# Context rows of the expert layer: ScalarE scales the value row in place, GpSimd adds it to the sum, VectorE keeps only the dot products

## The reference

```python
def peer_ffn(h, wq, keys, u, v):
    q = (x @ wq).reshape(n, PEER_HEADS, 2, PEER_DQ // 2)
    s = jnp.einsum('nhcd,hckd->nhck', q, keys)
    ... # per token: 8 heads x top 16 of 128 x 128 experts -> e (n x 128), softmax -> g
    def one(args):
        xb, eb, gb = args
        a = jax.nn.gelu(jnp.einsum('tkd,td->tk', u[eb], xb))
        return jnp.einsum('tk,tkd->td', (a * gb), v[eb])
```

## Time and profile before

| what | value |
|---|---|
| median of the runs | 4517.55 us (4517.3 to 4519.25) |
| span of the profiled execution | 4512.0 us |
| busy: PE / PEld | 3440.8 us (76%) / 1749.3 us (39%) |
| busy: DVE | 2848.3 us (63%) |
| busy: ACT | 1418.0 us (31%) |
| busy: POOL | 1434.5 us (32%) |
| moved by DMA | 1508.18 MB, 334 GB/s over the span |

### The profile page before, as it was taken

One profiled execution on the slowest core, in us unless ns is written; L12 is line 12 of the kernel. 1 busy time (PEld: TensorE's weight loads), 2 busy tenths in 40 slices (PEclk: granted clock), 3 DMA queues, 4 the chain that ended last, 5 costly groups with the idle time before them and its releaser, 6 DMA issues.

```text
span 4512.0 us, 39214 instructions
## 1 busy us (share of the span) xinstructions
PE 3440.8 (76%) x12464; PEld 1749.3 (39%) x12464; DVE 2848.3 (63%) x5950; ACT 1418.0 (31%) x4518; POOL 1434.5 (32%) x1306
## 2 busy tenths in 40 slices
PE   7888777666788778887777977788677777777776
PEld 3567554332443333432222466534232322323222
DVE  1227886777745765665675688758774675674544
ACT  2213554332223322222223345533222222222222
POOL 1000443233333333333333233222343343343332
PEclk9999788888999999999998988899899999999999
DMA  7443986668999999999997676556899999999997
GB/s 260 168 161 138 386 316 242 231 253 338 390 407 410 408 395 393 397 398 419 418 396 303 230 260 246 193 196 231 349 403 420 417 415 418 418 404 417 416 421 291
DMA packets 229119, 1508.18 MB, mean 334 GB/s; under 512 B 25392, under 2 KB 27440, under 8 KB 63920
## 3 DMA queue, kind: packets, MB, share of 16 engines
q0 software_dynamic: 185504, 1353.53, 75.2%
q1 hardware_dynamic: 43408, 152.14, 9.1%
HBM read 1501.38 MB, written 4.19 MB: 334 GB/s over the span
## 4 chain that ended last, share of the span: by engine, by line
DMA 34%; PE 33%; DVE 18%; ACT 8%; issue 6%; POOL 0%; SPq 0%; DVEq 0%; ACTq 0%; POOLq 0%
DMA work<-expert_dram,work 32%; PE psum L855 17%; DVE work L1688 5%; DVE work L1727 4%; PE psum L883 3%; PE psum L702 3%; PE psum L706 2%; DVE work L1737 2%; PE psum L770 2%; PE psum L795 1%; ACT work L1207 1%; ACT work L1220 1%; PE psum L754 1%; ACT work L1223 1%; DVE stat L1484 1%
## 5 line engine op out<-in xcount | busy, mean ns | idle before, releaser
L855 PE MATMUL psum<-work 128*128 128x512 f32 x4096 | 1958.6, 624 | 650.2 <-ACT work L1207 649.9
L1688 DVE SCALAR_TENSOR_TENSOR work<-work,psum 128x1024 f32<-128x1024 f32 x1024 | 1247.8, 1220 | 1026.3 <-DMA work<-expert_dram,work 1022.0
L1930 POOL DMA_INDIRECT work<-expert_dram,work x1024 | 995.6, 972 | 1726.9 <-PE psum L855 1683.1
L855 PEld LDWEIGHTS psum<-work 128*128 128x128 f32 x4096 | 767.7, 197 | 1804.9 <-ACT work L1207 1005.8
L1912 POOL DMA_INDIRECT work<-expert_dram,work x256 | 409.8, 1601 | 1209.4 <-DVE work L1727 804.8
L1198 ACT ACTIVATE work<-work 128x2 f32<-128x2 f32 x512 | 104.1, 203 | 1949.4 <-DVE work L1688 1949.3
L1727 DVE SCALAR_TENSOR_TENSOR work<-work 128x1024 f32<-128x1024 f32 x254 | 325.2, 1280 | 197.9 <-ACT work L1223 197.8
L1207 ACT ACTIVATE work<-const,work 128x128 f32<-128x128 f32 x1024 | 347.4, 386 | 0.7 <-PE psum L855 0.7
L1737 DVE SCALAR_TENSOR_TENSOR work<-work 128x1024 f32<-128x1024 f32 x256 | 311.8, 1218 | 11.7 <-DMA work<-expert_dram,work 11.7
L770 PE MATMUL psum<-work 128*128 128x128 f32 x1456 | 221.8, 312 | 73.2 <-ACT work L1130 60.6
L809 PE MATMUL psum<-work,ring 128*128 128x512 f32 x512 | 240.2, 625 | 28.1 <-ACT work L1077 28.1
(11 more groups left out here) (198 smaller groups left out, 2891.8 us busy)
## 6 DMA issues: line engine op xcount, KB each, us to landing
ring<-w_mod_dram SPq DMA_DIRECT2D x96, 512.0 KB, 5.2
ring<-w_in_dram SPq DMA_DIRECT2D x80, 512.0 KB, 5.3
ring<-w_query_dram SPq DMA_DIRECT2D x64, 512.0 KB, 5.5
work<-expert_dram,work POOLq DMA_INDIRECT x1280, 8.4
ring<-w_out_dram SPq DMA_DIRECT2D x32, 512.0 KB, 5.9
work<-rpb_dram POOLq DMA_DIRECT2D x2, 2688.0 KB, 12.3
xT<-xT_dram SPq DMA_DIRECT2D x1, 2560.0 KB, 11.2
work<-tables_dram POOLq DMA_DIRECT2D x2, 1024.0 KB, 5.4
```

The costliest lines, as they stand in the source:

```text
L855: last = pe.matmul(out[:, cols_], diag[:, n % NDIAG, :], rows[(SLOTS * t + s) % NBUF][:, D + 512 * half:D + 512 * half + 512], start=(s == ...
L1688: dve.scalar_tensor_tensor(u, u, 1.0, pair[0], ALU.mult, ALU.mult, accum_out=act_in[:, s:s + 1]).then_inc(dot_done, 1)
L1930: pool.indirect_dma_start(rows[m % NBUF], None, a[f"expert{l}"], bass.IndirectOffsetOnAxis(expert[:, t % 2, s:s + 1], 0)).then_inc(row_in[ ...
```

## The change

The weighted sum of step 4 leaves VectorE. ScalarE gets a fifth instruction for each slot: it multiplies the value row in its buffer by the coefficient, in place (128 x 1024), and waits for its own coefficient first. GpSimd then adds the scaled row to `csum` (a copy for slot 0). `ctx_work` on GpSimd issues what can be gathered, then an add, and after each add the gathers that this add makes possible. The rule by which a gather may be issued now looks at the adds that GpSimd has issued. VectorE's slot is the dot product alone.

```diff
@@ ScalarE, ctx_slots
                     act.activation(ccoef[:, one], ctanh[:, one], ACT.Identity, bias=chalf[:, one],
                                    scale=chalf[:, one]).then_inc(ctx_coef, 1)
+                    v = crows[CTX_BUF[l][0][s]][:, D:2 * D]
+                    act.wait_ge(ctx_coef, SLOTS * l + s + 1)
+                    act.activation(v, v, ACT.Copy, scale=ccoef[:, one]).then_inc(ctx_scaled, 1)
                     yield
@@ VectorE, ctx_slots
-                def add(s):
-                    v = crows[CTX_BUF[l][0][s]][:, D:2 * D]
-                    dve.wait_ge(ctx_coef, SLOTS * l + s + 1)
-                    if s == 0:
-                        last = dve.tensor_scalar(csum, v, ccoef[:, 0:1], None, ALU.mult)
-                    else:
-                        dve.wait_ge(ctx_added, SLOTS * l + s)
-                        last = dve.scalar_tensor_tensor(csum, v, ccoef[:, s:s + 1], csum, ALU.mult, ALU.add)
-                    last.then_inc(ctx_added, 1)
                 for s in range(SLOTS):
-                    if s:
-                        add(s - 1)
                     b = CTX_BUF[l][0][s]
...
-                add(SLOTS - 1)
@@ GpSimd
+            def ctx_add(l, s):
+                v = crows[CTX_BUF[l][0][s]][:, D:2 * D]
+                pool.wait_ge(ctx_scaled, SLOTS * l + s + 1)
+                if s == 0:
+                    last = pool.tensor_copy(csum, v)
+                else:
+                    pool.wait_ge(ctx_added, SLOTS * l + s)
+                    last = pool.tensor_tensor(csum, csum, v, ALU.add)
+                last.then_inc(ctx_added, 1)
+                ctx_sums[0] = s + 1
+            def ctx_work(l, calls, sums):
+                ctx_gather(l, calls)
+                while ctx_sums[0] < sums:
+                    ctx_add(l, ctx_sums[0])
+                    ctx_gather(l, calls)
...
-                    if s > calls + NBUF - 1 or (before[s] is not None and before[s] > calls - 2):
+                    if s > calls + NBUF - 1 or (before[s] is not None and before[s] >= ctx_sums[0]):
...
-                pool.wait_ge(ctx_added, SLOTS * l + 1 + max(s for s in range(SLOTS) if CTX_BUF[l][0][s] > 2))
+                outer = max(s for s in range(SLOTS) if CTX_BUF[l][0][s] > 2) + 1
+                ctx_work(l, calls, outer)
+                pool.wait_ge(ctx_added, SLOTS * l + outer)
                 pool.dma_start(keys, a["keysT"][l]).then_inc(keys_in, 16)
```

More of the change, by code:

```diff
@@ L535, in build @@
         ctx_coef = sem("ctx_coef")
+        ctx_scaled = sem("ctx_scaled")
         ctx_added = sem("ctx_added")
@@ L1893, in _ @@
         def _(pool):
-            ctx_next = [0]
+            ctx_next, ctx_sums = [0], [0]
+            def ctx_add(l, s):
[13 more added lines that the diff above has]
+                    ctx_gather(l, calls)
             def ctx_gather(l, calls):
@@ L1936, in _ @@
                 calls = 0
-                ctx_next[0] = 0
+                ctx_next[0] = ctx_sums[0] = 0
                 if l:
@@ L1958, in _ @@
                     if calls:
-                        ctx_gather(l, calls)
+                        ctx_work(l, calls, calls - 1)
                 for k in range(NPAIR):
@@ L1971, in _ @@
                     calls += ROW_CALLS[l]["Q"][s]
-                    ctx_gather(l, calls)
-                assert ctx_next[0] == SLOTS
+                    ctx_work(l, calls, calls - 1)
+                assert ctx_next[0] == SLOTS and ctx_sums[0] == SLOTS
                 gather(l)
```

2 lines of the change are left out of this document (removed).

## The result

The changed kernel is slower. It takes 4553.27 us (median of 6 runs, 4535.41 to 4574.58) against 4522.57 us of the kernel before in the same runs. The ratio is 1.007 with a 95% interval of 1.0043 to 1.0098. I had forecast 4490 us, which is 0.6% faster.

The account below looks back on a forecast made before the run. It took a loop of waits between VectorE and ScalarE, 3.73 us a slot, as the bound. Terms -10 - 5 + 0 - 13 - 5 + 0 + 2 + 4 = -27 us on 4512.0 gave 4485, plus 5.5 4490 us; range 4472 to 4508.

Parts of the forecast that it names:

- The place of the loop: Context slots: dot product, coefficient, sum and next dot product wait in turn on VectorE and ScalarE, 3.73 us a slot.
- the 250 that I had named: Sign of being right: ScalarE's waits for dot products fall from 522 us to under 250.
- relief in full: Rival: ScalarE's need alone decides; attention -32 and -29, out projection -9, queries -5; -75 us, 4443 us; chance 0.16.
- 2.0 to 2.7 us: Sign of being right: GpSimd's add takes about this long.
- The two paces, ScalarE's and GpSimd's: Attention, layer 0: ScalarE needs 8.6 us a step, GpSimd 8.5, against 9.67 us a step before.
- what is added on GpSimd: Step pricing GpSimd's 254 adds and 2 copies of 128x1024, beside its gathers: 3.75 us a slot.
- 1.738 x 1024/896 = 1.99 us undisturbed: GpSimd's add of 1024 columns, scaled from the same operation on 896 columns.
- I take 3.75, near the middle: GpSimd's time per slot in us, chosen between 3.3 at best and 4.1 with every dot product in the way.
- My upper end of 4.1: GpSimd's time per slot in us with every dot product in the way: 1.7 + 1.22 + (1.68 - 0.87) + 0.3.
- ScalarE's cost: Scaling on ScalarE, 1.05 us net; a slot costs 2.3 us, a step of attention in layer 1 6.6 us.
- slower: the shared path: Rival: GpSimd paces at 4.1 us a slot; attention, layer 0 unchanged, queries +25 and +7; about 4549 us; chance 0.24.
- the slower case: Outcome with GpSimd pacing, about 4549 us, chance 0.24; its sign was GpSimd with no idle time left in attention.

Follow-up runs that it names:

- the narrow add: The changed kernel with GpSimd's add cut to 64 of 1024 columns: 4420.95 us, ratio 0.9786 against the kernel before.
- the kernel without this: The changed kernel with attention's shares written as a tensor_scalar that also sums its output: 4532.15 us, ratio 1.0032 against the kernel before.

## Why the prediction was wrong

**Right.** The place of the loop: ScalarE's waits for dot products fell from 522 to 294 us, though not under the 250 that I had named, and the narrow add shows 4421 us, even below "relief in full". The add's length (2.356 us) lies in the "2.0 to 2.7 us" that I had named as a sign of being right, so that sign was too wide: the sum itself had 1.99. The scaling takes 1.148 us for 1.13. The two paces, ScalarE's and GpSimd's, were the right quantities to compare in attention of layer 0. Projection and out projection of layer 1 and the edge of the latent rows moved by less than 5 us.

**The step that failed** is "what is added on GpSimd", in two of its numbers:
- "1.738 x 1024/896 = 1.99 us undisturbed" is 2.356 us. The row it came from has an operand that is repeated eight times. The run with such an operand gives 1.970 us and 4497 us of time. I scaled by the number of elements and did not look at how the operands are read. The Trainium skill's "GPSIMD Engine Reference", section "3.1 Elementwise — side-by-side cycle accounting", has a figure for an add of two whole operands, 4497 ns for 2048 columns. Half of it, 2.25 us, is an estimate by that page, and it lies nearer to the trace than mine.
- "I take 3.75, near the middle" is 4.3 us. My upper end of 4.1 was built from 1.7 us of shared path; with the real add it is 2.36 + 1.21 + 0.82 = 4.4 us, and attention sits there, not in the middle: where GpSimd is the pace, dot products collect behind the add and run straight after it, in the way of the gather. The middle between "never meets" and "always meets" is no estimate for two engines in step. The sign that I had named for the slower case came: in 446 to 748 us GpSimd waits only 13.6 us in all for ScalarE (8.8 ahead of adds, 4.8 ahead of the first copy).

**What was missing:** the shares of attention. I listed dot products and the multiplications of the norm as what meets the adds. A tensor_scalar with one input I left out. The shares took 118 us more of VectorE in the two attention stages, and the kernel without this is about 21 us faster. In attention of layer 1 they and the dot products, not GpSimd's pace, lead the chain of waits: I had forecast -13 us there and 6.9 us more came.

**ScalarE's cost** was somewhat too small, which the other error hid: I had ScalarE at 6.6 us a step in attention of layer 1, and with the add over 64 columns the stage takes 279.4/40 = 7.0. The scaling costs 64 us there once the adds are out of the way (279.4 against 215.7).

The rival "slower: the shared path" had 4549 us at a chance of 0.24. It has the right mechanism and, for attention of layer 0, the right threshold: over 290/68 = 4.26 us a slot the stage grows, and 4.3 was measured. But it left attention as it was and laid all of its +32 us on queries, where 7 us came, against 19.8 in attention. That its time is so near to the measured 4553 is luck.

## What to carry to other kernels

Before an elementwise instruction goes from VectorE to GpSimd, list every VectorE instruction that will run beside it, those with two inputs from SBUF and plain tensor_scalar within SBUF, and add their durations to GpSimd's: here 1.28 us saved for each row cost 2.36 us of an add plus stalls of 0.66 us on each dot product. Price an operation by a row with the same kind of operands, not only the same number of elements. And where two engines wait for each other in turn, try first to swap two instructions in program order: that gave 1.8% here, where the move to two other engines lost 0.7%.

## What the runs showed of the hardware

- GpSimd's float32 add of 128 partitions takes 0.318, 1.273 and 2.356 us for 64, 512 and 1024 columns, 2.12 ns a column; with the second operand repeated eight times 1.970 us for 1024.
- A write of zeros by GpSimd takes 1.808 us for 2048 columns and stretches no dot product of VectorE that reads two tensors from SBUF.
- VectorE's tensor_scalar of 128x128 within SBUF (0.29 to 0.35 us) waits for a whole GpSimd add (up to 3.155 us), also when its recorded start is up to 0.7 us ahead of the add's, during the gather just before it; the form that also sums its output doesn't (0.345 to 0.348 us).
- GpSimd's indirect gather takes 1.64 and 1.78 us beside dot products that read two tensors from SBUF, and ends 0.82 us after them; beside those that read one input from PSUM it takes 0.972 us on average.
- ScalarE's scaling of 128x1024 float32 within SBUF by a column takes 1.148 us, and none of the 256 is longer than 1.154.
